# One block for projections, recurrent stage and query/key norms, with the modulation product on GpSimd

## The reference

```
h = rmsnorm(x, norm1_g)
qa, ka, va, iq, ik, iw, qb, kb, vb, g_lr, r_gate = split(h @ w_in)
qa, ka = rmsnorm(qa per head of 64, q_norm_g), rmsnorm(ka per head of 64, k_norm_g)
o_a = dsa_attention(...)      # an indexer scores all keys of a query with iq, ik, iw; the 128 best
                              # are kept; softmax attention over these, with a distance bias
log_a = log_sigmoid(g_lr @ gla_gate_w2 + gla_gate_b) / 16
for each chunk of 64 tokens, 4 heads (key 64, value 128):        # gla_chunked
    b = cumsum(log_a in the chunk)
    o = (q * exp(b)) @ state + (masked, decayed q k^T) @ v
    state = exp(b_last) * state + (k * exp(b_last - b))^T @ v
o_b = rmsnorm(o, gla_out_norm_g) * silu(r_gate)
x = x + concat(o_a, o_b) @ w_out; x = x + hier_moe(rmsnorm(x))
...
mod = silu(c) @ w_mod + b_mod                # second block; 1024 x 6144, for one row
```

## Time and profile before

| what | value |
|---|---|
| three timed executions | 2237.74 us median, 2227.49 to 2242.28 |
| the profiled execution | 2225.43 us, of which the span is 2223.7 us |
| PE busy | 1929.0 us (87%) |
| DVE / ACT / POOL busy | 1286.1 / 950.8 / 305.8 us |
| projection stage | 22 to 275 us |
| recurrent stage, `gla` | 276 to 377 us |
| `qk_norm` | 378 to 401 us |
| first attention, from | 402 us |

### The profile page before, as it was taken

One profiled execution on the slowest core, in us unless ns is written; L12 is line 12 of the kernel. 1 busy time (PEld: TensorE's weight loads), 2 busy tenths in 40 slices (PEclk: granted clock), 3 DMA queues, 4 the chain that ended last, 5 costly groups with the idle time before them and its releaser, 6 DMA issues. The chain is left out here.

```text
span 2223.7 us, 27035 instructions
## 1 busy us (share of the span) xinstructions
PE 1929.0 (87%) x8296; PEld 1353.6 (61%) x8296; DVE 1286.1 (58%) x2329; ACT 950.8 (43%) x1614; POOL 305.8 (14%) x243
## 2 busy tenths in 40 slices
PE   7989835995799999489998998779999999999993
PEld 3533325675677766357776887547766666666661
DVE  1796334642677777326436324437777777677763
ACT  2201131532465655336445322226655555555552
POOL 0000000400222222100000000011222222222221
PEclk9799955996799999789999999689999999999997
DMA  3438311044499988301211225417999999999983
GB/s 110 151 116 310 111 43 39 4 180 142 149 328 335 332 317 304 113 14 39 77 43 39 88 101 208 152 49 279 338 342 329 323 326 341 322 336 325 320 294 99
DMA packets 120321, 437.44 MB, mean 197 GB/s; under 512 B 31712, under 2 KB 36208, under 8 KB 83120
## 3 DMA queue, kind: packets, MB, share of 16 engines
q1 hardware_dynamic: 92552, 402.69, 48.8%
q0 software_dynamic: 27648, 33.67, 6.9%
q10 hardware_dynamic: 40, 0.05, 0.0%
HBM read 442.51 MB, written 63.48 MB: 228 GB/s over the span
## 5 line engine op out<-in xcount | busy, mean ns | idle before, releaser
L1448 DVE TENSOR_TENSOR big_parts<-big,h_cols_parts 128x1024 fp32r<-128x1024 f32 x384 | 459.4, 1222 | 99.5 <-ACT h_cols_parts L1501 91.8
L1501 ACT ACTIVATE h_cols_parts<-big 128x1024 fp32r<-128x1024 f32 x384 | 395.0, 1059 | 74.1 <-PE bank L1409 60.3
L1438 PE MATMUL bank<-big,heads 128*128 128x512 f32 x768 | 352.8, 602 | 1.5 <-ACT heads L1509 1.5
L1407 PE MATMUL bank<-h_cols_parts,heads_parts 128*128 128x512 f32 x768 | 311.8, 406 | 8.5 <-DVE heads_parts L1469 7.9
L1409 PE MATMUL bank<-h_cols_parts,heads_parts 128*128 128x512 f32 x768 | 302.9, 394 | 0.0
L1408 PE MATMUL bank<-big_parts,heads_parts 128*128 128x512 f32 x768 | 301.9, 393 | 0.0
L1712 POOL DMA_INDIRECT acc_scratch<-heads,small x96 | 158.5, 1652 | 629.6 <-DVE small L1479 391.9
L1438 PEld LDWEIGHTS bank<-big,heads 128*128 128x128 f32 x768 | 138.3, 190 | 139.8 <-issue 137.8
L1534 ACT ACTIVATE heads<-bank 128x512 f32<-128x512 f32 x96 | 57.4, 598 | 363.6 <-DMA acc_scratch<-heads,small 288.0
L1407 PEld LDWEIGHTS bank<-h_cols_parts,heads_parts 128*128 128x128 f32 x768 | 146.9, 191 | 39.3 <-DVE heads_parts L1469 8.7
L1409 PEld LDWEIGHTS bank<-h_cols_parts,heads_parts 128*128 128x128 f32 x768 | 145.8, 190 | 32.0
(11 more groups left out here) (362 smaller groups left out, 2852.1 us busy)
## 6 DMA issues: line engine op xcount, KB each, us to landing
big<-in_w_exp_down_dram SPq DMA_DIRECT2D x96, 1024.0 KB, 13.6
big<-in_w_exp_gate_dram SPq DMA_DIRECT2D x96, 1024.0 KB, 7.1
big<-in_w_exp_up_dram SPq DMA_DIRECT2D x96, 1024.0 KB, 13.8
big<-in_w_in_dram SPq DMA_DIRECT2D x13, 2048.0 KB, 8.2
heads<-in_w_mod_dram SPq DMA_DIRECT2D x6, 2048.0 KB
h_rows<-in_w_mod_dram SPq DMA_DIRECT2D x6, 2048.0 KB
big<-in_w_out_dram SPq DMA_DIRECT2D x4, 2048.0 KB, 10.7
h_scratch<-h_rows SPq DMA_DIRECT2D x8, 512.0 KB, 7.4
```

Of the source, the lines that this page charges most:

```text
L1407: pe.matmul(b_au[b][:, :], x_high, gu_high[:, :, c, :], start=c == 0, stop=False)
L1438: mm = pe.matmul(b_y[half][:, :], hidt[:, b, P * j:P * j + P], dn[q][:, j, 512 * half:512 * half + 512], start=j == 0, stop=j == FH - 1)
L1448: dve.tensor_tensor(gu_low[q][:, :, part, :], gu[q][:, :, part, :], gu_high[:, :, part, :].bitcast(F32), ALU.subtract).then_inc(w_low, 1)
L1501: act.activation(gu_high[:, :, part, :], gu[q][:, :, part, :], ACT.Copy).then_inc(w_high, 1)
```

## The change

The three stages become one block, `mixers` (L400 of the new kernel).

- Jobs now come in the order indexer, qb with kb, vb, q, k, rg, v. A unit of q, k, rg or v goes to banks 6 and 7 in turn; the recurrent stage has banks 0 to 5.
- The recurrent chunks stand between units: one chunk for each two units.
- Operands keep their layout: chunk c uses the rows of its own half of the partitions and heads use the halves of the feature tiles, so the copies to partition 0 (L677, L682, L724 and the doubled L719, L721, L723) are gone. The gate bias goes into ACT's copy, the state's scaling and addition become one instruction for each of two head pairs, the two parts of an output go to different banks and are added by DVE.
- The query and key norms are done as their rows come, and key and query are turned in pairs of heads, 4 transposes for each of 8 tiles (32 where there were 64). The query gain is folded into the key gain.
- The modulation product is on POOL, in 24 halves of 1 MB. For each block of 512 columns it has 8 multiplications (L841) and 7 additions (L844), each waiting for the one before. Its bias is added by PE: `mod_sum` is now two matmuls (L507, L508). One row buffer takes all 12 sums.
- The output gate's gain is multiplied on POOL at the block's end; scaling by the norm and the gate product are moved to POOL in the first attention, 8 instructions, one after every fourth unit.
- The offset ring of `attention` has 6 places instead of 8.

Core of the diff, shortened:

```diff
+        K.spare = sb("spare", 2 * D)
+        K.mod_row = sb("mod_row", 512, parts=1)
...
-    for c0 in (0, 512, 1024, 1832, 2344, 2872):
+    for c0 in (1832, 2344, 0, 512, 2872, 1024):
         job(cols("w_in", c0, 512, 0, 512))
...
+    loop_bank = lambda: 6 + len(copies) % 2
...
+            def mod_sum(bank=None):
                 j = len(mod_at)
+                pe.wait_ge(mod_used, 2 * j + 2)
+                out = claim(len(copies) % 8 if bank is None else bank)[0:1, :]
+                pe.matmul(out, K.ones[:, 0:1], mod_acc[j % 2], start=True, stop=False)
+                mm = pe.matmul(out, K.ident[0:MODS, j:j + 1], mod_bias, start=False, stop=True)
...
+            for c in range(NCH):
+                job, first = divmod(2 * c, T)
...
+                if first == 0:
+                    w = chunked(take_job(K, pe), KC, 512)
+                rows(f"{name}{first}", w, first, dest, loop_bank(), func)
+                if c + 1 < NCH:
+                    add_state(c)
+                    scores(c + 1)
+                rows(f"{name}{first + 1}", w, first + 1, dest, loop_bank(), func)
+                if first + 2 == T:
+                    end_job(K)
+                outputs(c)
+                if c in (3, 5):
+                    n = (c - 3) // 2
+                    pe.wait_ge(normed, n + 1)
+                    for i in range(4):
+                        turns(f"pair{n}{i}", [qk_rows[n][:, t, P * i:P * i + P] for t in range(T)],
+                              (K.q_pairs, K.k_pairs)[n][:, i, :], loop_bank())
+                if c < 7:
+                    mod_sum(loop_bank())
...
+        @block.gpsimd
+        def _(pool):
+            step = K.pool.on(pool)
+            for k in range(2 * MODS):
+                j, half = divmod(k, 2)
+                w, acc = mod_w[k % 2], mod_acc[j % 2]
+                pool.wait_ge(mod_in[k % 2], 16 * (k // 2 + 1))
+                if half == 0 and j >= 2:
+                    pool.wait_ge(K.products, mod_at[j - 2])
+                for c in range(KC // 2):
+                    cond = K.cond[:, KC // 2 * half + c:KC // 2 * half + c + 1]
+                    first = half == 0 and c == 0
+                    ins = pool.tensor_scalar(acc if first else w[:, c, :], w[:, c, :], cond, None, ALU.mult)
+                    if not first:
+                        step(ins)
+                        ins = pool.tensor_tensor(acc, acc, w[:, c, :], ALU.add)
+                    if c < KC // 2 - 1:
+                        step(ins)
+                ins.then_inc(mod_used, 1)
+                pool.wait_ge(mod_used, k + 1)
...
+            load_mod(2, 4)
             load_jobs(K, sp, 1)
...
+            load_mod(4, 9)
+            sp.wait_ge(K.bias_out, 16)
+            sp.dma_start(K.bias_dram, bcast(K.bias_once, P)).then_inc(K.bias_spread, 16)
+            load_mod(9, 11)
             load_jobs(K, sp, 1)
...
+            load_mod(18, 21)
+            load_jobs(K, sp, 1)
+            load_mod(21, 2 * MODS)
...
+    RING = 6
...
+                if rest and i % 4 == 3:
+                    rest(pool, i // 4)
```

More of the change, by code:

```diff
@@ new lines, in claim, with finish, unit @@
+                bank_user[bank] = u
+                return K.bank[bank]
+            def finish(mm, name, *copy):
+                marks[name] = len(copies)
+                copies.append(copy)
+                unit_at.append(product(K, mm))
+            def unit(name, lhs_rhs, out_of, dest, bank=None, func=ACT.Copy, scale=1.0, bias=0.0):
+                out = out_of(claim(len(copies) % 8 if bank is None else bank))
+                for c, (lhsT, rhs) in enumerate(lhs_rhs):
+                    mm = pe.matmul(out, lhsT, rhs, start=c == 0, stop=c == len(lhs_rhs) - 1)
+                finish(mm, name, dest, out, func, scale, bias, None)
@@ new lines, in columns, with rows, turns @@
+            def columns(name, w, c0, n, dest, scale=1.0):
+                unit(name, [(w[:, c, c0:c0 + n], K.ht[:, c, :]) for c in range(KC)], lambda b: b[0:n, :], dest, scale=scale)
+            def rows(name, w, t, dest, bank=None, func=ACT.Copy):
+                unit(name, [(K.ht[:, c, P * t:P * t + P], w[:, c, :]) for c in range(KC)], lambda b: b[:, :],
+                     dest[:, t, :], bank, func)
+            def turns(name, srcs, dest, bank=None):
+                out = claim(len(copies) % 8 if bank is None else bank)
+                for t, src in enumerate(srcs):
+                    mm = pe.transpose(out[:, P * t:P * t + P], src, K.ident[:, :])
+                finish(mm, name, dest, out[:, :], ACT.Copy, 1.0, 0.0, None)
@@ new lines, in square @@
+            def square(src, dest, after):
+                if after:
+                    act.wait_ge(sums, after)
+                act.activation(dest, src, ACT.Square).then_inc(squares, 1)
+            act.wait_ge(K.bias_out, 16)
+            copy_until(f"score{len(score_units) - 1}")
+            act.wait_ge(*taken_by("gate1"))
+            step(act.activation(kd, z, ACT.Abs))
+            step(act.activation(kd, kd, ACT.Exp, scale=-1.0))
+            act.activation(kd, kd, ACT.Ln, bias=K.ones[:, 0:1]).then_inc(gate_mid, 1)
@@ L507, in _, with pick @@
             step = K.dve.on(dve)
+            picked = [0]
+            def pick(rounds):
+                for _ in range(rounds):
+                    t, n = picked[0] // (TOPK // 8) + 1, picked[0] % (TOPK // 8)
+                    if t == T:
+                        return
+                    score = K.keep[:, t, 0:P * (t + 1)]
+                    if n == 0:
+                        diagonal = score[:, P * t:P * t + P]
+                        step(dve.tensor_tensor(diagonal, diagonal, K.causal[:, S - P:S], ALU.add))
+                    step(dve.max(top8, score))
+                    step(dve.match_replace(score, top8, score, TAKEN))
+                    if n == TOPK // 8 - 1:
+                        step(dve.tensor_scalar(score, score, TAKEN, MASKED, ALU.not_equal, ALU.mult))
+                    picked[0] += 1
@@ L534, in _ @@
[L534 to L543 removed]
+            pick(8)
@@ new lines, in _ @@
+            dve.wait_ge(gate_mid, 1)
+            step(dve.scalar_tensor_tensor(out=z, in0=z, scalar=0.0, in1=kd, op0=ALU.min, op1=ALU.subtract))
+            step(dve.tensor_scalar(z, z, 1.0 / 16.0, None, ALU.mult))
+            for j in range(2):
+                step(dve.tensor_tensor_scan(cum[:, j, :], reset, z[:, j, :], 0.0, ALU.mult, ALU.add))
+            by_chunk = lambda a: a.rearrange("p j (c s) -> p (j c) s", s=C)
+            cb = by_chunk(cum)
+            mid = cb[:, :, C // 2 - 1:C // 2].broadcast_to([P, 2 * NCH, C])
@@ L840, in attention @@
-def attention(K, tag, dim, out_col, bias=None, keep=None, loads=()):
+EXP_LIMIT = 80.0
+def attention(K, tag, dim, out_col, bias=None, keep=None, loads=(), heads=None, rest=None):
     nc = K.nc
```

667 lines of the change are left out of this document (322 added, 345 removed).

## The result

The changed kernel takes 2173.74 us (median of four runs, 2172.23 to 2176.87) beside 2232.61 us (2223.68 to 2242.28) for the kernel before on the same chip: a ratio of 0.9737, with an interval of 0.969 to 0.9785. It is faster by 59 us where the forecast was 90 us. The profiled execution took 2176.87 us with a span of 2175.1 us, and the profiled one of before 2225.4.

What follows compares the result with a forecast made beforehand. No engine bounded 275 to 402 us; engines waited for each other in turn. PE's merged stream summed to 311.7 us before the attention instead of 402, saving 90 us: 2237.7 - 90 = 2148 us, range 2122 to 2188.

Steps and rivals of the forecast that it cites:

- the case that I called likeliest: POOL stays below its allowance in the merged block and PE's clock is full; 2130 to 2160 us, chance 0.62.
- the first rival: POOL becomes the bound in the merged block through its modulation product; 2150 to 2183 us, 2171 at 22.7 a block, chance 0.17.
- my 2135: Whole kernel: 90 us saved from the profiled execution of 2225.4 us.
- my 2148: Whole kernel, the forecast itself: 90 us saved from the earlier median of 2237.7 us.
- The four waits of the earlier trace: PE's waits for normed queries 28.8, recurrent operands 27.1, small vectors 12.8 and modulation product 16.2 us; together 84.9 us.
- PE's stream: PE's work added step by step up to the attention, which would begin at 311.7 us and not at 402.
- The price of POOL's multiplication: Modulation product on POOL: 0.60 to 1.27 us for each multiplication, taken as 0.8, giving 17.1 us a block.
- The rule for the bound: Modulation product on POOL: each microsecond over 20.4 for a block costs PE 10.
- the allowance of 20.4: Time in us POOL may take for each of ten modulation blocks between PE's first and twelfth sums.
- Contention with DVE: DVE's two-input work slows POOL in the merged block: 1.8 us more a block, another 5 if picks count too.
- The clock: Rival: narrow work lowers PE's clock in each of seven loop turns, costing 14 to 28 us; 2160 to 2176, chance 0.1.
- What would show it: Signs in the new profile: attention at 312 us, loop clock 1.00, no PE wait for POOL's sums, ACT's copies 19 us apart.

Runs made afterwards that it cites:

- the probe: Changed kernel with an extra stage in front that times POOL's multiplications and additions alone and beside single kinds of DVE instructions; 2324.42 us, one execution.
- first experiment: Changed kernel with 84 of POOL's 96 modulation multiplications left out, so the product is not the reference's; 2132.7 us, ratio to the kernel before 0.9578.

## Why the prediction was right or wrong

The time of 2173.7 us is inside the range, but the case that I called likeliest did not come. The one that came was the first rival, POOL as the bound.

That the median lies beside that rival's 2171 is in part luck. In the trace the attention began 36.3 us later than in my sum, and the rest took 5.5 us more: with my 2135 for such an execution that is the 2176.9 of the profiled one. From my 2148 the 36 us alone would give 2184. But 2148 stood on a median of 2237.7 us of three executions of the kernel before, and later medians were 2228 to 2233.

- **What bounded the kernel before: right.** The four waits of the earlier trace rows were what could be got. The merge alone removes 93 us.
- **PE's stream: right, with small terms too large.** Forecast 311.7, measured 304.0 with POOL out of the way. A turn was put at 18.9 and is 18.29: two units 13.93, the sum 1.89, so a chunk is 2.5 instead of 3.1. A turn with the transposes of four pairs takes 224.87 - 203.81 = 21.06 in the same trace, so these cost 2.8 and not 3.2. Eight chunks and two such turns are 5.6 of the 7.7 us.
- **The price of POOL's multiplication: the step that failed.** I bounded it by a select of one tile (0.60) and the addition (1.27) of the earlier trace rows and took 0.8. It is 1.56, above the upper bound: "it costs no more than the addition" rested on the number of operands, and no row showed it. The gap of 0.09 us was near the 0.12 taken, the addition exactly 1.27. A block came to 22.7 us and not 17.1, which happens to be the upper end of my sum, since the 0.24 for each wait was as much too high there as the 1.27 for the multiplication was too low.
- **The rule for the bound: right.** I said that each microsecond over 20.4 for a block costs PE ten. With the measured 23.9 my own construction gives 82 + 10 x 23.9 + (2.0 + 17.0 + 6.7) = 346.7, and the attention began at 348.0. One number in it was wrong, not the model. I also had written the upper end, 22.7, beside the allowance of 20.4 and still gave this case 0.17: of my range of 13.7 to 22.7 a quarter lay beyond the line, and with my own 1.8 us for DVE's two-operand work added it is 4.1 of 9 us. By such a count the case deserved 0.25 to 0.45.
- **Contention with DVE: the mechanism is there, the size is small here.** Undisturbed blocks are 22.7 us, the ten in a row 23.9, so DVE's share is 1.2 (the slow ones, a multiplication of up to 3.67 us, lie beside DVE's two-operand steps and its scaling; I had 1.8 for two-operand work and 5 more if picks counted too). The picks don't count: MAX8 is 691 ns as in the earlier trace rows, and beside it POOL runs at its own pace. The Trainium skill, page "GPSIMD Engine Reference", section "Specifications", names as contending those DVE instructions that have two SBUF inputs or run in a 2-port mode; the probe's trace agrees, with 11.9 us alone against 15.5 beside two SBUF inputs; whether the one-input scaling (15.2) runs in such a mode, no row tells. Its DVE side I hadn't priced: the two scans take 1.66 us on average for the 1.22 of the earlier trace rows, and two-operand steps of 128x1024 up to 2.20. That cost PE nothing in the changed kernel, since DVE waited 26.0 us for PE's first scores.
- **The clock: fell, without cost in the loop.** In place of 1.00 the trace shows 0.91 and 0.90; without the waits for POOL it is 0.97 and 1.00 (first experiment). The rival's reason, narrow work, is refuted: in the first experiment the same narrow work stands in each turn and the clock is 1.00. What it cost behind POOL's end lies behind the last sum (3.3 us) and at the head of the attention (3.0 us).
- **What was late next.** "What would show it" named a wait of PE for POOL in each turn as the sign of this rival; the trace has six such waits of 2.1 to 5.3 us, two ahead of the loop and four in its seven turns. The first turn has none, nor have the two with the pair transposes, since there PE itself takes 21 us at full clock. Also, ACT's copies of the chunk outputs are 17.8 to 27.5 us apart and not 19.
- **The Trainium skill's price.** From the Trainium skill, page "GPSIMD Engine Reference", section "Performance versus the Vector engine", I had cited 769 ns as the best case for 512 elements with one input, which lay beside my 0.8. The measured 1.56 is twice that, for this form of multiplication with one value per partition; the measurement decides. The same page of the Trainium skill says in "Key points" that elementwise work is about twice as fast on VectorE. That spoke against the change, and for a multiplication with addition, one instruction on DVE and two on POOL, it was too mild: 0.75 against 3.0 us.

## What to carry to other kernels

When work moves to an engine on which its instruction has never run in the trace, compare the upper end of its price with the allowance, and let the chance of "becomes the bound" follow from how much of the price's range lies beyond. If the engine turns out to be the bound, look at the form before the placing: one wide product with a broadcast operand did in 3.74 us what four narrow ones did in 6.2 and more, and brought back what was lost to POOL's pace; but look at the neighbour too, whose two-operand steps went from 1.5 to 4.5 us beside it. And before curing a low clock, ask whether the waits that cause it are themselves the bound: filling them with work raised the clock from 0.89 to 0.97, and the time stayed, because the engine waited for had ended no earlier.

## What the runs showed of the hardware

- GpSimd's multiplication of 128x512 by one value per partition takes 1.56 us, longer than its addition of two such tiles (1.27). As a product with a broadcast operand, 128x2048 takes 3.60 us alone and 3.74 on average in the kernel, 0.90 to 0.93 for each 512. While it ran, a two-operand product of DVE of 128x1024 took 4.65 us instead of 1.22.
- DVE's scaling with one operand in SBUF (128x1024, 0.69 us alone) slows POOL as much as two-operand work does, and takes up to 1.64 us itself.
- Behind PE's waits of 2.1 to 5.3 us the 512-column passes of the changed kernel fell to the lower of the two clock levels, at once or a few passes later, and in the loop the next unit took 8.3 to 10.1 us instead of 7.13. With three accumulators a wait of 1.73 us left the clock up, while behind one of 1.04 us a unit took 8.79.
- The change of stage cost PE 4.15 us in front of its next matmul. With 3.7 us of matmuls at the end of the stage before, PE stood still for only 0.52 us and kept its clock, but the next stage came no sooner.
